# A decoder layer with 32 experts: the per-layer products moved from expert 15 to expert 5, one loop of 25 experts, and the general path behind the loop

## What is computed

```python
h = rmsnorm(x, g_mix)
z = h @ w_in                                  # 1024 x 5184
o_a, o_b = nsa_mixer(...), dsa_mixer(...)     # two sparse attentions, 8 heads each
merged = sigmoid(ga) * (o_a @ w_branch_a) + sigmoid(gb) * (o_b @ w_branch_b)
x = x + merged @ w_out
# top 4 of 32 experts by biased router logits, softmax over the four
#   gu = xe @ w1[e] + b1[e]; clamp; act = (lin + 1) * gate * sigmoid(1.702 * gate); act @ w2[e] + b2[e]
x = x + moe_ffn(rmsnorm(x, g_ffn), ...)
x = x + sigmoid(rmsnorm(x, g_ple) @ w_ple_gate) * (p @ w_ple)      # p is 256 x 256
```

## Time and profile before

| | |
|---|---|
| median of 3 runs | 1221.12 us (1220.26 to 1221.61) |
| the profiled execution | 1221.16 us, span 1219.0 us |
| TensorE busy | 1149.2 us (94%) |
| VectorE, ScalarE, GpSimd busy | 272.3, 191.7, 34.8 us |
| HBM read | 446.71 MB, 370 GB/s over the span |
| chain that ended last | TensorE 69%, DMA 28% |
| mean granted clock of TensorE | 0.986 |

### The profile page before, as it was taken

One profiled execution on the slowest core, in us unless ns is written; L12 is line 12 of the kernel. 1 busy time (PEld: TensorE's weight loads), 2 busy tenths in 40 slices (PEclk: granted clock), 3 DMA queues, 4 the chain that ended last, 5 costly groups with the idle time before them and its releaser, 6 DMA issues.

```text
span 1219.0 us, 15142 instructions
## 1 busy us (share of the span) xinstructions
PE 1149.2 (94%) x6374; PEld 489.3 (40%) x6374; DVE 272.3 (22%) x784; ACT 191.7 (16%) x407; POOL 34.8 (3%) x49
## 2 busy tenths in 40 slices
PE   7999999999999999999989789999989898988998
PEld 4455544454333343333333333333333343333344
DVE  1474543253111121111111111111112111111112
ACT  1223445131111111111111100000000000000011
POOL 2122100000000000000000000000000000000000
PEclk9999999999999999999999989999999999999999
DMA  8934170979999999999999999999999999999990
GB/s 273 343 139 158 50 208 31 419 243 380 421 430 432 430 432 431 430 434 432 430 432 430 426 430 432 430 431 433 431 431 433 431 431 432 431 432 432 425 378 34
DMA packets 40315, 448.39 MB, mean 368 GB/s; under 512 B 7455, under 2 KB 10624, under 8 KB 26354
## 3 DMA queue, kind: packets, MB, share of 16 engines
q1 hardware_dynamic: 38686, 441.66, 86.8%
q0 software_dynamic: 1264, 5.27, 1.2%
q10 hardware_dynamic: 324, 0.86, 0.3%
HBM read 446.71 MB, written 4.22 MB: 370 GB/s over the span
## 4 chain that ended last, share of the span: by engine, by line
PE 69%; DMA 28%; ACT 1%; issue 1%; DVE 0%; ACTq 0%; DVEq 0%
PE ps L435 22%; DMA wbuf<-in_w_e 16%; PE ps L464 13%; DMA ring<-in_w_e 12%; PE ps L1531 7%; PE ps L1614 5%; PE ps L407 4%; PE ps L398 3%; PE ps L1737 2%; PE ps L1647 2%; PE ps L1668 2%; PE ps L1578 2%; ACT xres L584 1%; PE ps L454 1%; PE ps L1605 1%
## 5 line engine op out<-in xcount | busy, mean ns | idle before, releaser
L435 PE MATMUL ps<-ring,xres 128*64 128x512 f32 x1216 | 277.0, 611 | 17.7 <-DMA ring<-in_w_e 17.5
L435 PE MATMUL ps<-wbuf,xres 128*64 128x512 f32 x832 | 186.2, 602 | 9.6 <-DMA wbuf<-in_w_e 9.6
L647 DVE TENSOR_SCALAR oT<-ps 128x512 f32<-128x512 f32 x32 | 22.1, 692 | 703.3 <-PE ps L435 703.3
L435 PEld LDWEIGHTS ps<-ring,xres 128*64 128x64 f32 x1216 | 88.9, 141 | 194.5 <-issue 165.3
L464 PE MATMUL ps<-ring,xres 128*64 128x512 f32 x608 | 134.8, 595 | 12.5 <-ACT xres L584 12.5
L435 PEld LDWEIGHTS ps<-wbuf,xres 128*64 128x64 f32 x832 | 60.5, 138 | 127.7 <-issue 110.2
L464 PE MATMUL ps<-wbuf,xres 128*64 128x512 f32 x384 | 85.0, 595 | 8.1 <-ACT xres L584 8.1
L580 ACT ACTIVATE oT<-oT 128x512 f32<-128x512 f32 x30 | 18.9, 630 | 451.1 <-DVE oT L647 451.1
L1531 PE MATMUL ps<-wbuf,hT 128*128 128x512 f32 (+2 forms) x224 | 86.1, 542 | 0.0
L464 PEld LDWEIGHTS ps<-ring,xres 128*64 128x64 f32 x608 | 42.2, 137 | 91.8 <-issue 80.5
L407 PE MATMUL ps<-xres 64*128 64x512 f32 x256 | 63.6, 615 | 0.0
(11 more groups left out here) (251 smaller groups left out, 789.9 us busy)
## 6 DMA issues: line engine op xcount, KB each, us to landing
ring<-in_w_e SPq DMA_DIRECT2D x50, 4096.0 KB, 37.1
wbuf<-in_w_e SPq DMA_DIRECT2D x34, 4096.0 KB, 37.8
ring<-in_w_e SPq DMA_DIRECT2D x16, 2048.0 KB, 24.0
wbuf<-in_w_in SPq DMA_DIRECT2D x9, 2048.0 KB, 12.7
wbuf<-in_w_e SPq DMA_DIRECT2D x8, 2048.0 KB, 9.8
wbuf<-in_w_out SPq DMA_DIRECT2D x2, 2048.0 KB, 8.4
wbuf<-in_w_ple_gate SPq DMA_DIRECT2D x2, 2048.0 KB, 41.1
rel_rows_repeated<-rel_rows POOLq DMA_DIRECT2D x1, 3072.0 KB, 20.4
```

What stands on the lines that cost most here:

```text
L435: l = mm((G, Lb)[n // 2][(n % 2) * SLOTS:(n % 2 + 1) * SLOTS, :], xeT[:, k, :], dealt(slots[at][:, r * 2 * DFF:(r + 1) * 2 * DFF])[n], sta ...
L647: d.tensor_scalar(gc, ps[0][:, :], LIMIT, None, ALU.min).then_inc(s["gc_ready"], 1)
```

## The change

The PLE stage moves from behind expert 14 to behind expert 4 (`PLE_AFTER` 5 for 15), ahead of TensorE's first loop. With that, TensorE has one loop over five groups (experts 5 to 29) in place of two and three. `w_ple` is loaded into `hT` once the router has read its first half of the transposed rows, and `p` into the part of `misc` where the per-head gains and the router's weights lay; both leave the ring, and `position` goes: piece n stands in slot n % 10. The four copies of the products are split, two to ScalarE and two to VectorE, and the fourth product has a bank of its own, the down products' bank. The decision moves behind expert 29 on all four engines. On TensorE the test is turned round: the usual branch holds the last pair and the last stage, the other holds the general path, then the last pair and the last stage a second time. New at the start of TensorE: 28 products (`WARM`) of a 64x64 output that nobody reads, from the constant `half`, behind the first memset. x3 and its transposes lie in slot 8 instead of slot 0.

```diff
-PLE_AFTER = 15
+PLE_AFTER = 5
-GATE_SLOTS = [(NE * PIECES + 2 + i) % NS for i in range(2)]
+GATE_SLOTS = [(NE * PIECES + i) % NS for i in range(2)]
+GENERAL_AT = PAIR * PIECES
+WARM = 28
...
-        ple_slot = Take(slots[PLE_AT % NS])
-        wple, pin, pT = ple_slot(2, DM), ple_slot(TT, PLE), ple_slot(2, SEQ)
+        p_words = misc[:, 569:1081]
+        pin, pT = p_words.rearrange("p (t d) -> p t d", t=TT), p_words.rearrange("p (k t) -> p k t", k=2)
+        wple = hT[:, :].rearrange("p (k n) -> p k n", k=2)
...
-                for j in range(ROUND):
-                    visit(j, lambda i: place_of(j * PIECES + i), j == 0)
-                with te.Fori(1, PLE_AFTER // ROUND) as g:
-                    five(g, 0)
-                ple_pe(te)
+                for j in range(PLE_AFTER):
+                    visit(j, lambda i: place_of(j * PIECES + i), j == 0)
+                ple_pe(te)
+
+                te.wait_ge(pl_ev, 3)
+                te.wait_ge(pl_right, 2)
+                with te.Fori(PLE_AFTER // ROUND, PAIR // ROUND) as g:
+                    for j in range(ROUND):
+                        visit(g * ROUND + j, lambda i: place(g, j, i))
+
+                def remaining():
+                    last_pair(PAIR, lambda i: place_of(PAIR * PIECES + i))
+                    finish()
+
                 n_max = largest(te)
-                with te.If(n_max > SLOTS):
-                    scatter_of(PLE_AFTER - 1).then_inc(flushed, 1)
+                with te.If(n_max <= SLOTS):
+                    remaining()
+                with te.Else():
+                    scatter_of(PAIR - 1).then_inc(flushed, 1)
                     expert_pe(te, rest)
-                with te.Fori(PLE_AFTER // ROUND, PAIR // ROUND) as g:
-                    five(g, 1)
-                last_pair(PAIR, lambda i: place_of(PAIR * PIECES + i))
+                    remaining()
...
                 if i == 3:
-                    te.wait_ge(pl_ev, 1)
+                    te.wait_ge(first["s"]["out_ready"], PLE_AFTER + 1)
...
-                    l = mm(ps[(0, 1, 3, 0)[i]][:, :], ...)
+                    l = mm(ps[(0, 1, 3, 2)[i]][:, :], ...)
...
-            for i in range(4):
-                sc.wait_ge(pl_ps, i + 1)
-                nc.scalar.copy(pl[:, i // 2, (i % 2) * 512:(i % 2 + 1) * 512], ps[(0, 1, 3, 0)[i]][:, :]).then_inc(pl_ev, 1)
+            sc.wait_ge(pl_ps, 5)
+            for i in (0, 2):
+                nc.scalar.copy(pl[:, i // 2, 0:512], ps[(0, 3)[i // 2]][:, :]).then_inc(pl_ev, 1)
+
+        def ple_dve(ve):
+            ve.wait_ge(pl_ps, 5)
+            for i in (1, 3):
+                nc.vector.tensor_copy(pl[:, i // 2, 512:1024], ps[(1, 2)[i // 2]][:, :]).then_inc(pl_right, 1)
...
                 sp.wait_ge(wo_ps, 4)
                 load_first(sp, 7)
+                sp.wait_ge(rt_ps, 1)
+                sp.dma_start(wple, io["w_ple"][0].rearrange("(k p) n -> p k n", p=P)).then_inc(ld_ple, 16)
                 sp.wait_ge(x2_taken, 1)
                 sp.wait_ge(xr_ready, 2)
...
                 sp.wait_ge(rt_ps, 2)
+                sp.dma_start(pin, io["p"][0, 0].rearrange("(t p) d -> p t d", p=P)).then_inc(ld_p, 16)
                 sp.wait_ge(hp_ready, 4)
                 load_first(sp, 9)
                 used = first["s"]["pieces_used"]
                 for n in range(NS, NE * PIECES):
-                    if n == PLE_AT:
-                        sp.wait_ge(used, PLE_AT - NS + 1)
-                        sp.dma_start(wple, ...).then_inc(ld_ple, 16)
-                        sp.dma_start(pin, ...).then_inc(ld_p, 16)
+                    if n == GENERAL_AT:
                         n_max = largest(sp)
                         with sp.If(n_max > SLOTS):
...
-                    if old == PLE_AT + 1:
-                        sp.wait_ge(pl_ps, 4)
-                    else:
-                        sp.wait_ge(used, old + 1 if old < PLE_AT else old - 1)
+                    sp.wait_ge(used, last - NS + 1)
...
             def _(te):
                 mm, tr = nc.tensor.matmul, nc.tensor.transpose
+                te.wait_ge(pool_ch, 1)
+                for _ in range(WARM):
+                    mm(ps[7][0:SLOTS, 0:64], half, half, start=True, stop=True)
                 te.wait_ge(ld_const, 16 * 4)
```

More of the change, by code:

```diff
@@ L323, in block_kernel, with place @@
         rest = dict(s=expert_sems("b"), piece=[sem(f"piece_b{i}") for i in range(PIECES)], col=NE, visits=(ROUNDS - 1) * NE, pre=0)
[L325 to L336, removed]
+        def place(g, j, i):
+            at = PIECES * j + i
             if at % 2:
                 return at % NS, None, 0
-            first_uses = 1 - (late and pair == PLE_AT % NS // 2)
-            return at % NS, piece[pair], g * (16 * ROUND * PIECES // NS) + 16 * (at // NS + first_uses)
+            return at % NS, piece[at % NS // 2], g * (16 * ROUND * PIECES // NS) + 16 * (at // NS + 1)
         def place_of(n):
[L344 to L347, removed]
+            pair = n % NS // 2
+            if n % 2 == 0:
+                return n % NS, piece[pair], 16 * (n // NS + 1)
             if n in WHOLE:
-                return pos % NS, None, 0
-            halves = [q for q in range(n + 1) if q not in WHOLE and position(q) % NS == pos % NS]
-            return pos % NS, piece[PAIRS + pair], 16 * len(halves)
+                return n % NS, None, 0
+            halves = [q for q in range(n + 1) if q not in WHOLE and q % NS == n % NS]
+            return n % NS, piece[PAIRS + pair], 16 * len(halves)
         def load(eng, e, i, at, signal):
@@ L364, in load_whole @@
             e, i = IN_ORDER[n]
-            pair = position(n) % NS // 2
+            pair = n % NS // 2
             src = w1[e, i // 2] if i < UP else w2[e]
@@ L591, in expert_act @@
                 ple_act(sc)
+                with sc.Fori(PLE_AFTER, PAIR) as it:
+                    visit(it)
                 n_max = largest(sc)
@@ L594, in expert_act @@
                     expert_act(sc, rest)
-                with sc.Fori(PLE_AFTER, PAIR) as it:
-                    visit(it)
                 sc.wait_ge(s["gc_ready"], PAIR + 1)
@@ L666, in expert_dve @@
                     visit(it)
+                ple_dve(ve)
+                with ve.Fori(PLE_AFTER, PAIR) as it:
+                    visit(it)
                 n_max = largest(ve)
@@ L669, in expert_dve @@
                     expert_dve(ve, rest)
-                with ve.Fori(PLE_AFTER, NE - 1) as it:
+                with ve.Fori(PAIR, NE - 1) as it:
                     visit(it)
@@ L678, in expert_dve @@
                 one_hot(slice(col, col + 1))
-                ve.wait_ge(first["s"]["sel_ready"], PLE_AFTER + 1)
+                ve.wait_ge(first["s"]["sel_ready"], PAIR + 1)
                 pick(slice(0, 1))
@@ L776, in _ @@
                     last = n + (n in WHOLE)
-                    old = position(last) - NS
-                    if old == PLE_AT + 1:
-                        sp.wait_ge(pl_ps, 4)
-                    else:
-                        sp.wait_ge(used, old + 1 if old < PLE_AT else old - 1)
+                    sp.wait_ge(used, last - NS + 1)
                     if n in WHOLE:
@@ L787, in _ @@
                 for i in range(2):
-                    sp.wait_ge(used, position(NE * PIECES) + i - NS - 1)
+                    sp.wait_ge(used, NE * PIECES + i - NS + 1)
                     sp.dma_start(wple_g[i], w_gate[:, 4 * i:4 * i + 4]).then_inc(ld_ple_gate[i], 16)
@@ L1720, in _ @@
                 take_x2(te, 1, 0)
-                expert_pe(te, first)
                 def x3_rows(t, m_):
@@ L1738, in gate, with last_stage @@
                     l.then_inc(g_ps, 1)
-                x3_rows(0, 0)
-                x3_rows(0, 1)
-                x3_rows(1, 0)
-                gate(0)
-                x3_rows(1, 1)
-                for i in range(1, len(GATED)):
-                    gate(i)
+                def last_stage():
+                    x3_rows(0, 0)
+                    x3_rows(0, 1)
+                    x3_rows(1, 0)
+                    gate(0)
+                    x3_rows(1, 1)
+                    for i in range(1, len(GATED)):
+                        gate(i)
+                expert_pe(te, first, last_stage)
 def constants():
```

33 lines of the change are left out of this document (14 added, 19 removed).

## The result

The changed kernel takes 1215.28 us (median of six runs, 1214.07 to 1216.84) beside 1220.76 for the kernel before on the same chip: a ratio of 0.9947 (0.9934 to 0.9961), 5.5 us less, where 1216.0 was forecast. The profiled execution took 1215.63 us with a span of 1213.7. These are the rows that answer to those of before. "The stream" is SyncE's queue of weight loads, and "the last pair" the pair of pieces that TensorE waits for at line 427 in expert 30 (its third piece).

What follows compares the result with a forecast made beforehand. The weight stream (DMA) was taken to bound the loop, TensorE the stretches before it and after its last wait. From 1221.16, -1.8 -3.0 -0.5 = -5.3, plus 0.2 for the tail's clock, gave 1216.0 us; range 1213.8 to 1219.0.

Steps and rivals of the forecast that it cites:

- The front: TensorE's start: WARM keeps the clock up, so transposes and first products finish sooner; -1.8 us, ends -2.3 and +4.
- w_ple and p: Loads leave the DMA-bound stream for gaps near 270 and 273, free there; -3.0 us, ends -3.0 and 0.
- The PLE products behind expert 5: Products early in the loop: 9.7 us without a weight piece used, hidden by the DMA queue; 0.
- The decision: Behind visit 29: test at most 0.9 us, under the 1.27 wait, no jump on the usual path; 0, ends 0 and 6.2.
- One loop body less: TensorE's loop: the second body's 8 instruction packets no longer take stream time; -0.5 us, ends 0 and -1.5.
- The total: Whole kernel: -1.8 -3.0 -0.5 = -5.3, plus 0.2 for the last stretch's clock; forecast 1216.0 us.
- The tail's clock: After the last wait for weights: half clock for one stretch or not, 0 or +1.7 us; taken as 0.2.
- Rival (b): TensorE's loop: a body touching eight pages plus one fetched ahead would miss on every pass; chance 0.12.

Runs made afterwards that it cites:

- undone version: Changed kernel with w_ple and p loaded ahead of piece 22, in the full stream, instead of ahead of the loop: 1219.07 us, ratio 0.9977.
- the other order: Changed kernel with TensorE testing for the general path and jumping over it, the usual path following once: 1217.65 us, ratio 0.9961.
- shifted loop: Changed kernel, WARM kept, with 36 idle instructions behind each of the first five visits, 180 in all, ahead of the loop: 1222.73 us, ratio 1.0016.
- two_bodies: Changed kernel with TensorE's loop over experts 5 to 29 written as two loops of two and three groups: 1217.39 us, ratio 0.9964.
- second profile: The changed kernel, unaltered, measured again beside the variants: 1215.66 us, ratio 0.9951.
- first kernel without WARM: Changed kernel without WARM and with nothing in its place, so the loop body starts 112 instructions sooner: 1223.86 us, ratio 1.0027.
- no_warm_padded: Changed kernel with WARM's products replaced, at the same place, by 224 waits (112 instructions) on a semaphore already there: 1223.2 us, ratio 1.0022.
- no_warm_layout: Changed kernel without WARM, with 28 idle instructions behind each of visits 0 to 3, so the loop keeps its place: 1216.44 us, ratio 0.9965.

## Why the prediction was right

Forecast -5.2 against its own profile, measured -5.5 by the medians and -5.35 at the last step. By its steps:

- **The front**, -1.8: measured -1.65 between the two profiles (278.71 to 277.06). Transposes 1.70 instead of 1.8, the first product at 10.08, 1.41 earlier instead of 1.3, and its 32 records in 8.24 us instead of the 7.9 of the forecast, so 0.25 saved and not 0.5. WARM by itself gave 0.8 to 1.5, as the constants land and as the clock rises without it.
- **w_ple and p**, -3.0 in the stream and 0 at the new place: the undone version costs 3.4 by medians; by bytes at 404 the loads are worth 2.2 to 2.9 us. The mechanism is right; the 0 of the new place holds within 0.8 us.
- **The PLE products behind expert 5**, 0: no gap in DMA, 2.4 us of copies' waits all hidden, TensorE waiting for weights again at 668, about visit 14. Right.
- **The decision**, 0: right as written, and right for the reason given, since the other order shows an idle time of 2.80 us. Its upper bound, 6.2, was too high for this place: the jump there cost 1.5 to 2.0 us.
- **One loop body less**, -0.5 with an end at -1.5: mis-sized, the weakest step. Its 430.4 GB/s counts the packets' own 0.13 MB as if they were weights; the weights alone moved at 429.5, 0.7 us by the same sum. The two kernels' bytes in 560:1120 say 1.2 us for the eight packets. The shifted loop charges 0.18 to 0.19 us a packet, 1.5 for eight; two_bodies' 1.7 for six would be 0.28 each, but is within the noise. So 1.2 to 1.5, inside its range and well over twice its mean.
- **The total** is near the forecast partly by luck, since two errors cancel: front and loads together put the stream 3.9 us ahead (4.3 in the second profile) and not 4.8, and the packets gave 1.2 and not 0.5. What makes 3.9 of 4.8 is not tested; the stream's jitter of up to 1 us between runs of one kernel is as large.
- **The tail's clock**, +0.2 between 0 and 1.7: both cases happened to the same kernel. The dear one costs 1.4, and came with a pair that landed 1.1 earlier, so it doesn't show between these two profiles.
- **Rival (b)**, 0.12: its mechanism is real, its price the dear one (0.19 a packet), and only the place decides. Counted by the program's order (the count on record in the expectations), the body is 6.45 stretches of 16 KB, the size of a packet; in the changed kernel it begins just inside a stretch and touches seven. 180 instructions later, or with 112 fewer ahead, it touches eight, and is fetched on every pass. The starting place in a stretch is an estimate from these counts and from where packets came in the runs; no row shows it. Five runs bear it out: packets on every pass in the shifted kernel, in the first kernel without WARM and in the kernel before with WARM, and none in the two kernels where 112 other instructions take WARM's place ahead of the loop (no_warm_padded, no_warm_layout).

The Trainium skill (Runtime: NRT & Kernel Launch, Instruction fetch mechanics) says that a long kernel need not fit, since crossing a 16 KiB boundary is mostly hidden. In the straight code of the changed kernel that holds: its list of waits has none by issue. For the packets of a loop that is fetched on each pass, in a stream that is already full, it doesn't hold: 37 packets, 7.1 us.

## What to carry to other kernels

Before an edit that adds or removes instructions of TensorE ahead of a loop is judged by its own worth, count where the loop body then starts: here 180 instructions that do nothing cost more than the whole change had gained. Look at the instruction packets in the later passes; there should be none. In a stretch that DMA bounds, move bytes to a stretch with gaps; time saved on an engine there is worth nothing until the stream ends. Put the usual branch next in order. A decision where the array still has some microseconds of queued work may cost less; here that is argued, not tested.

## What was not expected of the hardware

- An instruction packet costs the stream more than its bytes. 33 packets, 0.54 MB, are 1.3 us at 430 GB/s. Their own time is 0.4% of 560 us on 16 engines, 2.2 us, 0.07 each. The weights' queue moved 1.40 MB less in that window (240.46 against 241.86), 3.2 us, 0.10 each. The time grew by 0.19 each. A possible reading is that a piece is complete only when the slowest of 16 engines is, and a packet delays one of them; that was not tried.
- Waiting instructions on TensorE whose semaphore is long there are not free: 112 of them, two waits each, took until 13.04 from about 0.95, when their semaphore came in the other kernels: 0.11 us each.
- The filler of 28 products took 6.18 and 6.16 us in the two profiles of the changed kernel and 4.76 to 5.74 in seven profiles of other kernels. In all but one the constants landed later still. In the second profile of the changed kernel they were there when the filler ended, at about 7.1, and yet it cost nothing: the first product waited 0.53 us for its weights.
